# Summing blocks of decays on GpSimd before the ones product of the mixer's denominator

## The reference, cut to what matters

```python
D = b[..., :, None] - b[..., None, :] + ic[..., None, :]
D = jnp.where(tril, D, -jnp.inf)
W = jnp.einsum('bhtd,bhsd->bhts', qc, kc) * jnp.exp(D - m_t[..., None])
num = jnp.einsum('bhts,bhsv->bhtv', W, vc) + w_int[..., None] * jnp.einsum('bhtd,bhdv->bhtv', qc, C)
den = jnp.sum(W, axis=-1) + w_int * jnp.einsum('bhtd,bhd->bht', qc, n)
h = num / jnp.maximum(jnp.abs(den), jnp.exp(-m_t))[..., None]
```

## Time and profile before

| | |
|---|---|
| time, median of 3 runs | 1778.87 us (1776.03 to 1781.55) |
| time of the profiled execution | 1776.79 us |
| its span, first to last instruction | 1775.0 us |
| PE busy | 1743.1 us, 98% |
| DVE, ACT, POOL busy | 1117.8, 1169.3, 381.6 us |
| mean granted TensorE clock | 0.997 |

### The profile page before, as it was taken

One profiled execution on the slowest core, in us unless ns is written; L12 is line 12 of the kernel. 1 busy time (PEld: TensorE's weight loads), 2 busy tenths in 40 slices (PEclk: granted clock), 3 DMA queues, 4 the chain that ended last, 5 costly groups with the idle time before them and its releaser, 6 DMA issues.

```text
span 1775.0 us, 26517 instructions
## 1 busy us (share of the span) xinstructions
PE 1743.1 (98%) x10204; PEld 1441.1 (81%) x10204; DVE 1117.8 (63%) x1918; ACT 1169.3 (66%) x1719; POOL 381.6 (21%) x457
## 2 busy tenths in 40 slices
PE   9997999999999999999999999999999999999999
PEld 7875787778787887989989776767777879899897
DVE  6998567756747677637446466696754467275372
ACT  6788768666666776747647775666575667476473
POOL 2787012332322111111111111100101111111111
PEclk9999999999999999999999999999999999999999
DMA  8898678666565787787887976545656877878877
GB/s 248 190 213 183 168 195 217 158 168 156 134 154 127 189 192 181 175 195 183 190 183 187 261 175 144 126 114 131 153 131 170 202 190 174 202 172 194 190 176 182
DMA packets 91693, 313.88 MB, mean 177 GB/s; under 512 B 12144, under 2 KB 12272, under 8 KB 90800
## 3 DMA queue, kind: packets, MB, share of 16 engines
q0 software_dynamic: 45488, 145.26, 43.2%
q1 hardware_dynamic: 43488, 156.00, 27.9%
q10 hardware_dynamic: 2592, 10.94, 1.7%
HBM read 160.88 MB, written 6.29 MB: 94 GB/s over the span
## 4 chain that ended last, share of the span: by engine, by line
PE 80%; DVE 9%; ACT 6%; DMA 4%; issue 1%; POOL 1%; ACTq 0%; DVEq 0%; POOLq 0%
PE ps L2147 48%; PE ps L2257 19%; PE ps L2164 3%; DMA w_lo<-w_raw 3%; PE ps L2222 2%; DVE ps L1693 2%; ACT w_hi L632 1%; ACT w_lo L646 1%; PE ps L2475 1%; PE ps L2487 1%; PE ps L2730 1%; PE ps L2691 1%; PE ps L2516 1%; PE ps L2775 1%; PE ps L2788 1%
## 5 line engine op out<-in xcount | busy, mean ns | idle before, releaser
L551 POOL DMA_DIRECT2D w_lo<-w_raw x289 | 247.7, 859 | 1317.0 <-ACT w_lo L646 1233.8
L632 ACT ACTIVATE w_hi<-w_raw 128x1024 fp32r<-128x1024 f32 (+1 forms) x289 | 288.6, 999 | 140.9 <-PE ps L2147 124.2
L2147 PE MATMUL ps<-H_hi,w_hi 128*128 128x512 f32 x680 | 277.9, 409 | 10.0 <-DMA w_lo<-w_raw 8.6
L2147 PE MATMUL ps<-H_lo,w_hi 128*128 128x512 f32 x680 | 265.0, 390 | 0.0
L2147 PE MATMUL ps<-H_hi,w_lo 128*128 128x512 f32 x680 | 264.9, 390 | 0.0
L646 ACT ACTIVATE w_lo<-w_raw 128x1024 fp32r<-128x1024 f32 x253 | 264.8, 1046 | 0.0
L2147 PEld LDWEIGHTS ps<-H_hi,w_hi 128*128 128x128 f32 x680 | 127.7, 188 | 47.2 <-issue 13.4
L1383 DVE SCALAR_TENSOR_TENSOR X<-ps,X 128x512 f32<-128x512 f32 (+1 forms) x68 | 49.2, 723 | 174.8 <-PE ps L2147 166.9
L2147 PEld LDWEIGHTS ps<-H_lo,w_hi 128*128 128x128 f32 x680 | 127.8, 188 | 31.3 <-issue 6.5
L2147 PEld LDWEIGHTS ps<-H_hi,w_lo 128*128 128x128 f32 x680 | 127.6, 188 | 27.1
L2147 PE MATMUL ps<-mid_hi,w_hi 128*128 128x512 f32 x352 | 137.3, 390 | 1.5 <-DVE mid_lo L1390 1.5
(11 more groups left out here) (423 smaller groups left out, 4079.2 us busy)
## 6 DMA issues: line engine op xcount, KB each, us to landing
w_raw<-weights SPq DMA_DIRECT2D x289, 512.0 KB, 4.3
w_lo<-w_raw POOLq DMA_DIRECT2D x253, 512.0 KB, 5.4
w_lo<-w_raw POOLq DMA_DIRECT2D x36, 256.0 KB, 4.7
pl_P<-spill ACTq DMA_DIRECT2D x1, 2048.0 KB, 9.6
spill<-X ACTq DMA_DIRECT2D x8, 256.0 KB, 5.8
X<-spill ACTq DMA_DIRECT2D x2, 1024.0 KB, 5.9
out<-X SPq DMA_DIRECT2D x8, 256.0 KB, 3.7
at_pair<-at_raw POOLq DMA_DIRECT2D x96, 16.0 KB, 2.3
```

The source lines that it names most:

```text
L551: pool.dma_start(w_lo[:, u, 0:width], w_raw[:, u, 0:width], accum_op=ALU.add).then_inc(lo_landed[u], 16)
L632: return act.activation(out_ap, in_ap, ACT.Copy)
L2147: mm = pe.matmul(ps[:, bank, :], w, x, start=first and n == 0 and q == 0, stop=last and n == len(blocks) - 1 and q == 2, skip_group_check= ...
```

## The change

In phase 2 of each head PE no longer multiplies all four blocks with ones. POOL adds the blocks b = 1, 2 and 3 into a new buffer `ml_D` (384, 256 and 128 columns), and PE makes two ones products in place of four: one of the first 128 columns of block 0, one of the 384 columns of `ml_D`. The numerator's four products stay. The first add also takes in columns 128 to 511 of block 0. Each add waits for its block (`kq_done`) and for the add before it. In POOL's stream the adds of a head stand right behind `low` of the tile that ACT prepares in the head's phase 2. The first add of a later head waits for the sums of the head before; PE's last product waits for the third add.

```diff
@@ GpSimd @@
+            def add_decays(h):
+
+                for b in range(1, NQ):
+                    pool.wait_ge(kq_done, NQ * h + b + 1)
+                    block, total = key_block(b), ml_D[:, P * b:S]
+                    if b == 1:
+                        if h:
+                            pool.wait_ge(sums_made, h)
+                    else:
+                        pool.wait_ge(decays_added, (NQ - 1) * h + b - 1)
+                    pool.tensor_tensor(total, ml_E[:, P:S] if b == 1 else total, ml_E[:, block], ALU.add)\
+                        .then_inc(decays_added, 1)
+
+            steps = TILES0[9] + 13
             for n in range(first + 4 * SLOTS, sum(TILES)):
                 low(n)
+                h, phase = divmod(n - steps - AHEAD, 3)
+                if phase == 2 and 0 <= h < MH:
+                    add_decays(h)
@@ TensorE @@
                     for b in range(NQ):
                         pe.wait_ge(kq_done, NQ * h + b + 1)
-                        for bank, w in ((2, ml_U[:, 4 + h, b * P:(b + 1) * P]), (3, ones)):
-                            mm = pe.matmul(ps[:, bank, P * b:S], w, ml_E[:, key_block(b)], start=b == 0,
-                                           stop=b == NQ - 1, skip_group_check=True)
-                    mm.then_inc(sums_made, 1)
+                        pe.matmul(ps[:, 2, P * b:S], ml_U[:, 4 + h, b * P:(b + 1) * P], ml_E[:, key_block(b)],
+                                  start=b == 0, stop=b == NQ - 1, skip_group_check=True)
+                    pe.matmul(ps[:, 3, 0:P], ones, ml_E[:, 0:P], start=True, stop=True, skip_group_check=True)
+                    pe.wait_ge(decays_added, (NQ - 1) * (h + 1))
+                    pe.matmul(ps[:, 3, P:S], ones, ml_D[:, P:S], start=True, stop=True, skip_group_check=True)\
+                        .then_inc(sums_made, 1)
```

More of the change, by code:

```diff
@@ L262, in build @@
                                             ("ml_E", [P, 10 * P], F32))
+                _, _, _, ml_D = scope(("ml_NM_", [P, S], F32), ("ml_NMd_", [P, NQ, P], F32), ("ml_E_", [P, 10 * P], F32),
+                                      ("ml_D", [P, S], F32))
             ya_hi, ya_lo = keep("ya_hi", [P, 4, S], F32R), keep("ya_lo", [P, 4, S], F32R)
@@ L340, in build @@
         kq_made = sem("kq_made")
+        decays_added = sem("decays_added")
         kq_done = sem("kq_done")
```

## The result

| | before | after |
|---|---|---|
| time, median (lowest to highest), 12 runs each | 1776.83 us (1773.59 to 1781.55) | 1779.30 us (1777.10 to 1782.27) |
| time of the profiled execution | 1776.79 us | 1780.81 us |
| its span | 1775.0 us | 1778.8 us |
| mean granted TensorE clock in it | 0.997 | 0.993 |

The ratio of after to before is 1.0019, 95% interval 1.0010 to 1.0028: +3.4 us (1.8 to 5.0); the two medians differ by 2.5. The kernel became slower, by less than the 0.3% that the prediction took as visible, an outcome to which it gave 0.53. Forecast were 1785.1 us and +6.2 us. The time lies in the range given, the step is 40 to 55% of the one forecast.

What follows compares the result with a forecast made beforehand. PE and DVE were taken to run level through heads 1 and 2, with ACT setting POOL's issue. -1.29 + 2.07 + 1.8 + 2.98, plus 0.6 for the clock, gave +6.2 on 1778.9: 1785.1 us, range 1777 to 1789.

Steps and rivals of the forecast that it cites:

- Head 0, -1.29: At head 0 the adds are hidden and everything behind PE's sum of squares comes 1.29 us earlier.
- Adds on POOL, 1.03, 0.78 and 0.52: Times in us forecast for POOL's adds of 384, 256 and 128 columns; 2.67 together with two gaps.
- The fifth that doesn't go by columns: Share of a 512-column instruction's time independent of columns, read from DVE's line and used for POOL's adds.
- Turns in heads 1 and 2, 2.07 + 1.8: POOL's adds and DVE's two-operand SBUF operations exclude each other, delaying DVE's chain 2.07 us in head 1, 1.8 in head 2.
- an add ends, a waiting DVE operation of 0.69 starts: Rule for the exclusion: DVE's whole 0.69 us operation follows POOL's add, and the next add waits for it.
- Head 2's product would wait 0.5 to 1.5 for POOL: In head 2 PE's last ones product waits 0.5 to 1.5 us for POOL's adds.
- 1.7: PE's wait at 1174 us for the square grows from 0.4 to about 1.7 us.
- Head 3, +2.98: In head 3 the adds stand behind POOL's issue and, with exclusion, PE ends its products 2.98 us later.
- Clock, +0.6: Behind PE's idle time in head 3 the last product runs at half speed, 0.6 us; possible price nothing to 4.2.
- here weight tiles follow without one, so I stay near the lower end: Reason for the small clock charge at head 3: weight tiles follow without a gap, unlike the work after the earlier wait.
- no turns: Rival: SBUF reads of POOL and DVE don't exclude each other; +0.7 us, 1779.6; chance 0.41.
- All hidden: Rival: the adds are hidden in all four heads; about -2.2 us, 1776.7; chance 0.02.

Runs made afterwards that it cites:

- e3: The changed kernel without POOL's adds; the second ones product reads block 0's columns 128 to 511; 1772.28 us, ratio 0.9992 to the kernel before.
- e5: The change in heads 0 and 3 only, head 3's adds ahead of POOL's issue, heads 1 and 2 as before; 1771.01 us, ratio 0.9978 to before.
- e1: The kernel before plus POOL's twelve adds, whose result nobody reads; PE keeps four ones products a head; 1778.34 us, ratio 1.0036.
- e7: The changed kernel with each POOL add replaced by a memset of the same columns; run once, 1773.64 us.
- e6: The changed kernel unaltered, timed and profiled once more; 1778.93 us, ratio 1.0020 to the kernel before.
- e10: The changed kernel plus eight PE products of 4 columns, two a head; 1780.97 us, ratio 1.0020 to the kernel before.
- e2: The changed kernel with head 3's adds ahead of the weight tile's DMA issue in POOL's stream; 1773.03 us, ratio 1.0004 to the kernel before.
- e8: The changed kernel with each POOL add replaced by a copy of one block; run once, 1776.17 us.
- e9: The kernel before plus eight PE products of 4 columns, two a head; 1776.75 us, ratio 1.0001 to the kernel before.

## Why the prediction was off

Point by point, against the sum on record:

- **Head 0, -1.29.** As forecast. The adds of 384 columns and of 256 and 128 together took 1.33 and 1.35 us and were hidden. DVE ran L1920 and L1921 (MAX8 and MATCH_REPLACE8 of 256 columns) beside them, at 0.42 and 0.41 us, as it does without them (before, e3).
- **Adds on POOL, 1.03, 0.78 and 0.52.** Measured alone 1.01, then 1.34 for the other two with the gap (e5). The fifth that doesn't go by columns, taken over from DVE, was a good guess, and the bounds were far too wide.
- **Turns in heads 1 and 2, 2.07 + 1.8.** Right in kind, and the choice that the rows left even: e1 shows them with the adds alone, e7 shows that without POOL's reads there are none. Too large in size, 1.24 + 1.06. The step that failed is "an add ends, a waiting DVE operation of 0.69 starts": the waiting operation ends 0.55 us after the add, and of the add that waits for it in turn only 0.59 us lie behind DVE's operation, where it takes 0.74 alone. By the Trainium skill, "SBUF — State Buffer", section "SBUF: two separate sides", the pair of ports is held for the whole instruction, and the other engine blocks fully. That they block each other the traces bear out, and also that POOL has to read SBUF for it (0 lost by DVE beside memsets). That it lasts for the whole record they do not quite: DVE's operation ends 0.55 us behind the record of an add or a copy, with one read or two, and not 0.69. It loses 0.69, 0.41 and 0.14 us where the sum had 0.83, 0.75 and 0.49.
- **Head 2's product would wait 0.5 to 1.5 for POOL.** It didn't. The clock had fallen near 1174 us behind PE's wait of 2.9 us for the square, which I had put at 1.7 and had not thought able to lower the clock. The 1.7 were 0.4 + 1.29 and left out that DVE is late by head 1's turns; with their 1.24 it makes 2.9. PE was late itself, and the adds were there.
- **Head 3, +2.98.** Measured 2.59; the wait was 4.4 us with "about 4 to 5" forecast. The adds are over 3.88 us behind the start of the issue where the sum had 4.58, by the size of the turns, which lie on this path too; the product behind them takes 0.91 where it had 0.65.
- **Clock, +0.6.** Measured 2.40 in the profile of after (0.74 in the product, 1.66 in the tiles), 1.56 in that of e6, none in e10. The step that failed is "here weight tiles follow without one, so I stay near the lower end". Dense work didn't bring the clock back at once. The earlier trace rows had the better figure, half of a stretch of low clock, and 4.2 stood in the text as the upper bound.

The misses cancel: 2.58 + 2.98 + 0.6 = 6.2 forecast, 1.05 + 2.59 + 2.40 = 6.04 in the profile. That the sum came out right there was luck, and no proof of its terms. Turns in heads 1 and 2 were put 1.6 us too high, head 3 0.4 too high, the clock 1.0 to 1.8 too low, which makes 5.2 to 6.0 us in the part. The rest lies elsewhere: the 1.4 us that came back near 1450 us were in no term, since I costed the edit only where it stands. With them it is 3.8 to 4.6 us, and +3.4 (1.8 to 5.0) was measured. Whether the usual run loses less to the clock than the two profiled ones isn't shown; their mean granted clock, 0.993 and 0.994, is in the middle of the twelve runs' 0.991 to 0.994. Last, the median of 3 runs from which I started lay 2 us above that of 12, and it was added to the forecast of the time.

The rival "no turns" (+0.7) would have given nearly the same verdict, and only the rows of DVE tell it from the truth. "All hidden" (-2.2 forecast) is refuted for the change, and e2 and e5 show what it takes: e2 with the adds placed early has +0.41, since the turns of heads 1 and 2 stay, and e5 without those has -1.92.

What stays open: why the clock is low for 5.1 us behind a wait in after, 3.4 in e6 and not at all in e10, and what links the length of PE's stream to a weight tile's arrival. For e2 and e3 the local length and the 1.4 us would make -1.0 and -3.3 us, and the medians say +0.7 (-1.1 to 2.5) and -1.4 (-3.5 to 0.9): inside the intervals, but these are too wide to confirm the 1.4.

## What to carry to other kernels

Moving work from a full engine to an idle one pays only where the full engine is the last to be waited for, and only if the idle one can start in time: its queue, here one issue that waited for ACT, cost 4 to 5 us, and the move was worth 2. Before placing work on GpSimd that reads SBUF, with one operand or two, look at what DVE does in the same microseconds; in head 0, beside DVE's MAX8 and MATCH_REPLACE8, the same adds cost nothing. And a new pause of TensorE has to be priced at its length plus a stretch at half clock behind it (0 to 2.4 us here), even when dense work follows.

## What the runs showed of the hardware

- An add of 384 columns on GpSimd with both inputs in SBUF takes 1.01 us alone; those of 256 and 128 take 1.34 with the gap between them. Beside two-input operations of DVE the two take 1.87.
- DVE's operation of 512 columns with two SBUF inputs (0.69 us alone) took 1.20 to 1.51 when it met the add of 384 columns, 1.10 behind that of 256, 0.83 behind that of 128; 0.69 beside memsets, 0.69 to 1.00 beside copies. Where it had to wait it ended 0.54 to 0.56 us behind the end of GpSimd's record, with an add and with a copy alike.
- The granted clock of TensorE was at half behind waits of 1.6 us (e1, e3, e7), 1.9 us (e8), 2.4 us (e10), 2.9 us and 4.4 us (after), and at 1.00 behind one of 1.2 us (e8) and one of 3.5 us (e10). With the wait of 4.4 us it was low for 6.8 us in one profile, 5.1 of them behind the wait, and for 3.4 us in another of the same kernel.
- A float32 product of 384 columns with 128 rows took 0.65 us in a row of products and 0.91 behind a wait, at full clock; 1.65 behind a wait at half clock.
- A wait for a weight tile 0.2 ms behind the edit was 2.0 to 2.2 us or 0.7 to 0.9, as TensorE's stream had its old length or more (before, e1, e9, e10) or was shorter.
